# First column half of an output projection by k-pairs over four banks, with two seven-product chunks mixed into the residual

## What is computed

```python
y = jnp.concatenate([y_ret, y_mla, y_gm], axis=2)
y = rms_norm(y, mix_norm.reshape(N_MIX_HEADS, HEAD_DIM)).reshape(B, S, D_MIX)
y = jnp.concatenate([y[..., :RET_WIDTH] * jax.nn.silu(r_g), y[..., RET_WIDTH:]], axis=-1)
x = x + y @ w_out                      # 256 x 2048 @ 2048 x 2048
h = rms_norm(x, ffn_norm)
return x + (jax.nn.silu(h @ w_gate) * (h @ w_up)) @ w_down
```

## Time and profile before

| | us |
|---|---|
| median of 3 runs | 1089.78 (1089.72 to 1089.99) |
| the profiled execution | 1089.62 |
| its span | 1087.5 |
| busy in the span: PE | 1076.9 |
| busy in the span: DVE | 911.0 |
| busy in the span: ACT | 653.2 |

### The profile page before, as it was taken

The page is one execution under the profiler, slowest core; times in us unless marked ns, Lnnn a source line. Parts: engine busy times, 40 slices in busy tenths (PEclk is TensorE's granted clock), DMA queues, the critical chain, the costliest instruction groups (busy, mean ns, idle before and its releaser), DMA issues.

```text
span 1087.5 us, 12417 instructions
## 1 busy us (share of the span) xinstructions
PE 1076.9 (99%) x5094; PEld 897.1 (82%) x5094; DVE 911.0 (84%) x859; ACT 653.2 (60%) x638; POOL 55.4 (5%) x54
## 2 busy tenths in 40 slices
PE   9999999999999999999999999999999999999997
PEld 6888889987888877888888888888888888888886
DVE  6889666754576799999999999999999899989994
ACT  7666546655755566655656656566665655565653
POOL 0087000000000000000000000000000000000000
PEclk9999999999999999999999999999999999999999
DMA  8766544654355578677677677677684676655562
GB/s 327 281 212 227 192 135 133 205 161 147 117 189 167 188 271 271 198 233 243 216 232 229 209 237 222 226 232 221 229 246 155 208 257 242 202 205 202 194 198 111
DMA packets 50440, 227.50 MB, mean 209 GB/s; under 512 B 4305, under 2 KB 10193, under 8 KB 28753
## 3 DMA queue, kind: packets, MB, share of 16 engines
q1 hardware_dynamic: 48224, 214.89, 57.9%
q0 software_dynamic: 1440, 10.49, 4.7%
q10 hardware_dynamic: 720, 1.34, 0.3%
HBM read 222.51 MB, written 4.19 MB: 208 GB/s over the span
## 4 chain that ended last, share of the span: by engine, by line
PE 93%; DVE 3%; DMA 2%; ACT 1%; issue 0%; SPq 0%; DVEq 0%; ACTq 0%
PE ps L1680 72%; PE ps L1533 5%; PE ps L1535 5%; PE ps L1534 5%; PE ps L1572 2%; DMA d_raw<-in_w_gu 1%; PE ps L1620 1%; PE ps L1799 1%; PE ps L1800 1%; PE ps L1801 1%; DMA raw<-in_w_out 0%; PE ps L1619 0%; DMA raw<-in_w_i 0%; DVE ps L1375 0%; PE ps L1591 0%
## 5 line engine op out<-in xcount | busy, mean ns | idle before, releaser
L1680 PE MATMUL ps<-w_hi,xp_hi 128*128 128x512 f32 x404 | 159.6, 395 | 1.5 <-DVE ps L1375 1.0
L968 DVE TENSOR_TENSOR w_lo<-raw,w_hi 128x2048 fp32r<-128x2048 f32 (+2 forms) x42 | 87.3, 2078 | 84.1 <-ACT w_hi L493 84.1
L1680 PE MATMUL ps<-w_hi,xp_lo 128*128 128x512 f32 x404 | 157.5, 390 | 0.0
L1680 PE MATMUL ps<-w_lo,xp_hi 128*128 128x512 f32 x404 | 157.3, 389 | 0.0
L753 ACT ACTIVATE t_hi<-t_sum 128x2048 fp32r<-128x2048 f32 x44 | 84.4, 1919 | 69.9 <-DVE t_sum L1262 69.9
L836 ACT ACTIVATE w_hi<-raw 128x2048 fp32r<-128x2048 f32 (+1 forms) x44 | 79.1, 1798 | 77.6 <-DMA raw<-in_w_dn 77.6
L1680 PE MATMUL ps<-w_hi,xo_hi 128*128 128x512 f32 x292 | 113.9, 390 | 0.0
L1680 PE MATMUL ps<-w_lo,xo_hi 128*128 128x512 f32 x292 | 113.6, 389 | 0.0
L1680 PE MATMUL ps<-w_hi,xo_lo 128*128 128x512 f32 x292 | 113.6, 389 | 0.0
L1272 DVE TENSOR_TENSOR t_lo<-t_sum,t_hi 128x2048 fp32r<-128x2048 f32 x44 | 100.7, 2289 | 6.7 <-ACT t_hi L753 6.7
L493 ACT ACTIVATE w_hi<-raw 128x2048 fp32r<-128x2048 f32 (+2 forms) x42 | 73.0, 1739 | 53.0 <-DMA raw<-in_w_out 25.7
(11 more groups left out here) (294 smaller groups left out, 2446.0 us busy)
## 6 DMA issues: line engine op xcount, KB each, us to landing
raw<-in_w_gu SPq DMA_DIRECT2D x78, 1024.0 KB, 5.0
raw<-in_w_dn SPq DMA_DIRECT2D x44, 1024.0 KB, 4.8
raw<-in_w_i SPq DMA_DIRECT2D x21, 1024.0 KB, 4.8
raw<-in_w_out SPq DMA_DIRECT2D x16, 1024.0 KB, 5.1
raw<-in_w_in SPq DMA_DIRECT2D x12, 1024.0 KB, 5.1
d_raw<-in_w_gu SPq DMA_DIRECT2D x10, 1024.0 KB, 4.9
d_lo<-in_w_gu POOLq DMA_DIRECT2D x10, 1024.0 KB, 11.5
raw<-in_w_in SPq DMA_DIRECT2D x8, 576.0 KB, 3.8
```

Of the source, the lines that this page charges most:

```text
L968: nc.vector.tensor_tensor(w_lo[n % 4][:, 0:k, 0:c], raw[n % 4][:, 0:k, 0:c], w_hi[n % 4][:, 0:k, 0:c].bitcast(F32), ALU.subtract).then_inc ...
L1680: mm = nc.tensor.matmul(out, x, wt, start=start and j + m == 0, stop=stop and 3 * j + m == n - 1, skip_group_check=resumed)
```

## The change

The chunks 50 to 57, which before were the column blocks 0 and 1 in turn, are now one pair of k-tiles each, over both column blocks and both token blocks, in banks 0 to 3. The weights for them are laid out anew in memory (`w_oa`), so that a chunk's 128 rows are contiguous. Pairs 0 to 4 and 7 are plain (`out_plain`), pairs 5 and 6 (chunks 55 and 56) are seven-product chunks (`out_sums`). Their four shared products collect in banks 4 to 7. These banks are mixed in step 56 into a tile `mix_o`, and the mixture is added to `xin`, not to the banks. The chunks 58 to 65 run as before, but in banks 4 to 7. The units `xs2` and `xt2` of the feed-forward part take banks 0 to 3. In the first feed-forward chunk the order of the six early products is changed.

```diff
-OUT_ORDER = [(0, 0), (1, 0), (0, 1), (1, 1), (0, 2), (1, 2), (0, 3), (1, 3)] + [
-    (s, g) for s in (2, 3) for g in range(4)]
+O1 = O0 + FB
+OUT_SUMS = (5, 6)
+OUT_ORDER = [(s, g) for s in (2, 3) for g in range(4)]
...
-put(51, ("yt", 3), ("yt", 4), ("yt", 5))
-put(54, ("yt", 6), ("yt", 7))
+put(51, ("yt", 3), ("yt", 4), ("ys", 5))
+put(54, ("ys", 6), ("yt", 7))
...
         def unit_bank(u):
-            return bank[4 + INDEX[u] % 4]
+            return bank[INDEX[u] % 4 + (0 if u[0] in ("xt2", "xs2") else 4)]
...
+            def out_hi(n):
+                s = out_sum(n)
+                if s is None:
+                    high(n)
+                    return
+                act.wait_ge(raw_in[n % 4], 16 * (n // 4 + 1))
+                nc.scalar.activation(w_hi[n % 4][:, 1:4, :], raw[n % 4][:, 1:4, :], ACT.Copy).then_inc(hi_ready, 1)
+                act.wait_ge(in_sum_step, 3 * (in_weight_sums + s + 1))
+                nc.scalar.activation(to_hi[s][:], to_sum[s][:], ACT.Copy).then_inc(in_tops_hi, 1)
...
+            def y_sums_hi(s):
+                act.wait_ge(xi_step, 3 * (in_token_sums + s + 1))
+                nc.scalar.activation(yi_hi[s][:], yi[s][:, 4:8, :], ACT.Copy).then_inc(xi_sums_hi, 1)
+            y_sums_at = {52: 0, 55: 1}
-            x2_step = {55 + 1: 0, 57: 1, 61: 2, 65: 3}
+            x2_step = {57: 0, 58: 1, 61: 2, 65: 3}
...
+                if n in y_sums_at:
+                    y_sums_hi(y_sums_at[n])
+                if n == O0 + OUT_SUMS[-1]:
+                    act.wait_ge(in_mix_done, 5)
+                    nc.scalar.activation(mix_o[:, 0, :], bank[4], ACT.Copy).then_inc(in_mix_first, 1)
...
+            def out_lo(n):
...
+                nc.vector.tensor_tensor(to_sum[s][:, 0:2, :], raw[slot][:, 1:3, :],
+                                        b12.unsqueeze(1).to_broadcast([P, 2, COLS]), ALU.add).then_inc(in_sum_step, 1)
...
+            def y_sums(u):
...
+            def out_mix_sums():
...
+            y_sums_at = {52: 0, 55: 1}
-            out_step = {56: 0, 57: 1, 61: 2, 65: 3}
+            out_step = {61: 2, 65: 3}
             for n in range(G0, FF0):
+                if n == O1 - 1:
+                    dve.wait_ge(in_mixed, 6)
...
+                if n in y_sums_at:
+                    y_sums_lo(y_sums_at[n])
+                if n == O0 + OUT_SUMS[-1]:
+                    out_mix_sums()
...
-                    low(n + AHEAD)
+                    out_lo(n + AHEAD)
+                if n == O0 + OUT_SUMS[-1]:
+                    out_mix_x()
...
+            def out_sums(n):
...
+                shared = ((4, "a11", "b11"), (5, "n2", "t2"), (7, "s1", "t1"), (6, "s3", "t3"))
+                own = ((0, "a12", "b21"), (2, "s4", "b22"), (1, "a22", "t4"))
+                pe_.wait_ge(ys_lo, s + 1)
+                pe_.wait_ge(xi_made, in_token_sums + s + 1)
+                pe_.wait_ge(lo_ready, n + 1)
+                for out, left, right in own + shared if start else shared + own:
+                    if start and out == 4:
+                        after(unit_act, "a", ("yt", 7))
+                        after(unit_dve, "v", ("yt", 7))
...
+            for n in range(O1, FF0):
...
+                if n == O1:
+                    pe_.wait_ge(in_mix_first, 3)
+                    pe_.wait_ge(in_mix_step, 9)
...
-                for out, x, right in products[6:] if late else products[:6] if first and start else products:
-                    if first and start and out == 0:
+                if first and start:
+                    products = products[6:] if late else products[:2] + products[4:6] + products[2:4]
+                for out, x, right in products:
+                    if first and start and out in (4, 5):
+                        pe_.wait_ge(acc_free, ACC_O + out + 1)
+                    if first and start and out == 7:
                         late_units()
```

More of the change, by code:

```diff
@@ L166, in build @@
         mix_in = at("mix_in", 144 * K, [4, COLS])
+        to_sum = [at(f"to_sum{i}", 112 * K + 8 * K * i, [4, COLS]) for i in range(2)]
+        to_lo = [at(f"to_lo{i}", 112 * K + 8 * K * i, [4, COLS], F32R) for i in range(2)]
+        to_hi = [at(f"to_hi{i}", 128 * K + 8 * K * i, [4, COLS], F32R) for i in range(2)]
+        yi = [at(f"yi{i}", 64 * K + 4 * K * i, [8, P]) for i in range(2)]
+        yi_hi = [at(f"yi_hi{i}", 72 * K + 2 * K * i, [4, P], F32R) for i in range(2)]
+        yi_lo = [at(f"yi_lo{i}", 76 * K + 2 * K * i, [4, P], F32R) for i in range(2)]
+        mix_o = at("mix_o", 144 * K, [4, COLS])
         mix = at("mix", H0 + 44 * K, [4, COLS])
@@ L1284, in _ @@
                         cols = xin[:, b, s * COLS:(s + 1) * COLS]
[L1285 removed]
+                        nc.vector.tensor_tensor(cols, bank[2 * s + b][:], cols, ALU.add).then_inc(acc_free, 1)
                 if n == O0:
@@ L1817, in _, with out_plain @@
                 run_units(n)
[L1820 to L1825, removed]
+            def out_plain(n):
+                p, slot = n - O0, n % 4
+                after(unit_dve, "v", ("yt", p))
+                pe_.wait_ge(lo_ready, n + 1)
+                for side in range(4):
+                    half, b = divmod(side, 2)
+                    if p == 0 and half == 0:
+                        pe_.wait_ge(proj_free, 11 + b)
+                    elif p == 0:
+                        pe_.wait_ge(acc_free, ACC_G + 3 + b)
+                    toks, blocks = slice(b * P, (b + 1) * P), (1 - half, 3 - half)
+                    mm = group(bank[2 * half + b], [yT_hi[:, 2 * p + j, toks] for j in range(2)],
+                               [yT_lo[:, 2 * p + j, toks] for j in range(2)], [w_hi[slot][:, j, :] for j in blocks],
+                               [w_lo[slot][:, j, :] for j in blocks], p == 0, p == FB - 1)
+                    if p == FB - 1 and side < 3:
+                        mm.then_inc(in_done, 1)
+                    if side == 1 and n == MID:
+                        run_units(n)
+                mm.then_inc(chunk_used, 1)
@@ L1826, in _ @@
+            for n in range(O0, O1):
+                if out_sum(n) is None:
+                    out_plain(n)
+                else:
+                    out_sums(n)
                 if n != MID:
                     run_units(n)
+            y_made = {0: ("yt", 1), 1: ("yt", 3), 2: ("yt", 4), 3: ("yt", 7)}
+            for n in range(O1, FF0):
+                s, g = OUT_ORDER[n - O1]
+                after(unit_dve, "v", y_made[g])
+                if g >= 2:
+                    pe_.wait_ge(ys_lo, g - 1)
+                if n == O1:
+                    pe_.wait_ge(in_mix_first, 3)
+                    pe_.wait_ge(in_mix_step, 9)
+                chunk(n, yT_hi, yT_lo, range(4 * g, 4 * g + 4), 2 * s, g == 0, g == 3)
+                run_units(n)
```

118 lines of the change are left out of this document (110 added, 8 removed).

## The result

| | before | changed |
|---|---|---|
| median of the runs side by side, us | 1089.78 (1089.62 to 1090.55, 5 runs) | 1098.49 (1098.07 to 1099.61, 5 runs) |
| the profiled execution, us | 1089.62 | 1098.08 |
| its span, us | 1087.5 | 1095.6 |

The ratio is 1.0078, with a 95% interval from 1.0067 to 1.0089: the change makes the kernel 8.7 us slower. The forecast was 1097.7 in a range of 1095.1 to 1099.6.

A forecast was written before the change was run, and what follows sets the result against it. PE, busy 99% of the span, was taken as the bound. A 7.3 us wait less 1.36 saved gave +5.9, the clock +2.1: 1089.62 + 5.9 + 2.1 = 1097.6, as median 1097.7, range 1095.1 to 1099.6.

The forecast's parts named there:

- PE sets the time, and the saving is 1.36 us: Output projection: PE has no idle time; seven products instead of eight in chunks 55 and 56 save 1.36 us.
- DVE's program set out in time: DVE's instructions through steps 51 to 54, timed from rows: no pause from 311.7, reads of yt 7 done at 332.0.
- The stop: Chunk 55, after nine matmuls: PE waits before bank 4 for DVE's reads of yt 7, 7.3 us.
- The clock: Behind PE's wait in chunk 55: clock falls to its lower level, +2.1 us, between 0 and 3.
- No second stop: Chunk 56 on: mixing done by 340.7, before chunk 58; nothing more ends late, further waits taken as nothing.
- The clock holds: Rival, chunk 55: same wait but clock stays at 2.4 GHz, no slow stretch, 1095.7 us; chance 0.16.
- DVE is not late: Rival, reads of yt 7: done by 327.63 gives 1091.2 (short wait, chance 0.04), by 324.9 gives 1088.4 (covered, 0.02).
- More stops: Rival: slower preparations, or chunk 58 or units behind it wait; 1099 to 1103, chance 0.08 including a longer slow stretch.

The follow-up runs named there:

- experiment 1: Changed kernel with the new layout, banks and order but all eight pairs plain, no seven-product chunks: 1089.82 us, ratio 1.0000.
- experiment 8: Changed kernel's computation reordered: yt 7 read before the rest of chunk 56's and all of chunk 57's preparation, wait before bank 7: 1089.66 us, ratio 1.0002.
- experiment 7: The changed kernel itself, unaltered, run and profiled once more: 1099.00 us, ratio 1.0082.
- experiment 3: Changed kernel with yt 7 read ahead of pair 6's token sums, the wait before bank 4 being for both: 1096.76 us, ratio 1.0062.
- experiment 4: Changed kernel with the wait for yt 7 moved from before bank 4 to before bank 7: 1098.13 us, ratio 1.0074.
- experiment 5: Changed kernel without the two DVE instructions making the lo part of the weight sums, so its result is not the layer's: 1096.64 us, ratio 1.0061.
- experiment 2: Changed kernel with 31 extra matmuls put before the wait for yt 7 to keep PE at work: 1096.97 us, ratio 1.0064.
- experiment 6: Changed kernel with 16 or 23 extra matmuls before the wait for yt 7: 1098.46 us (ratio 1.0076) and 1098.69 us (1.0077).

## Why the prediction was right, step by step

- **PE sets the time, and the saving is 1.36 us.** Shown by experiments 1 and 8: with the layout alone nothing changes, and with the stop gone the stretch is 1.0 us shorter, the 1.36 less a wait of 0.2 and the slower matmuls behind it. What I left out is that such a saving need not last: in the medians of experiment 8, 0.6 of it is left at the end of the span and nothing in the device time.
- **DVE's program set out in time.** The prediction had `to_sum` at 312.3 and 320.5 and the reads of yt 7 done at 332.0. The trace has 312.12, 320.36 and 331.89. Every duration came from a row of the kernel before, and twenty instructions added up to an error of 0.1 us. As a time of day that is partly luck, for in experiment 7 the same program has everything 0.8 us later. Counted from the start of chunk 55 it is not: the restart was put at 9.35 us, and it came at 9.47 in both profiles. This works because DVE waits for almost nothing in these 20 us; an estimate by average load (DVE had 29 us to spare) would have said that there is no problem.
- **The stop.** 7.3 us forecast at nine matmuls into chunk 55, 7.14 measured there. DVE's lateness is 4.3 of it (its reads end at 331.89 instead of 327.63); the other 2.8 is that PE now asks earlier. Experiments 3 to 5 confirm its cause from three sides: fewer items before DVE's reads, the wait put later, less work on DVE. In each the restart moved as DVE's reads did, and stayed where only PE's order was changed.
- **The clock.** Taken at +2.1 from the start of the kernel; 2.2 measured, and 2.07 by experiment 2. The step from "PE comes from standing" to "PE has stood for 7 us" held. That the size fits so well is luck: the forecast took 4.5 us of slow matmuls from the start of the kernel, and the 4.5 behind this restart are what was left of a low stretch of 6.8 us, 2.3 of which had passed. The same program gave 1.6 in experiment 7, and the other kernels 1.6 to 2.9. The fall that the Trainium skill warns of for idle gaps in the middle of a kernel ("TensorE: Matmul & The Clock Gate", "Why this matters for your kernels") took place here, where PE stood 4.26, 5.56, 5.78, 7.14 and 7.15 us; in the profiles with 1.95 and 3.51 us it did not.
- **No second stop.** The mixing ended at 342.96 and chunk 58 came at 347.15, as predicted (347.3). The part behind it took 748.4 against 748.3 us.
- **The rivals.** "The clock holds" falls by the intervals of 0.43 us. "DVE is not late" falls by its timeline; experiment 8, where DVE reads yt 7 in time, ended at the kernel before's time and not near 1088.4, for the reasons given there. "More stops" does not show in the profile of the changed kernel, but its twin, waits in the feed-forward part that come and go, showed in experiments 5, 6 and 8.

The forecast was 0.8 us low by the median. Of this, 0.1 is the sum inside the span (+8.1 measured, +8.0 predicted). About 0.4 lies outside the span: the profiled execution is 2.5 us longer than its span, where I had carried over the 2.12 of the kernel before. In all executions with seven-product chunks in this place that part is 2.36 to 2.75 us, in all without them 2.04 to 2.16. What it consists of the profile does not show, and no run was spent on it. The remainder is that the median lies 0.4 above the profiled execution, where before it lay 0.16 above, and the clock's share and the waits in the feed-forward part, which vary as the table shows, can account for that. That they do is not shown.

## What to carry to other kernels

Before an engine with idle time on average is given more work, set its program out in time with durations from the trace and ask for the one moment at which somebody waits for it; here 29 us of spare time hid a stop of 7 us. A wait in the middle of a chunk for "all units up to the last" is as late as the latest reader, so the reader should stand before the new preparation, not behind it. Where the effect is near 1 us, compare a stretch between two marks on the bounding engine rather than the medians.

## What was not expected of the hardware

- The clock fell while PE still stood, 3.5 to 4.8 us after its last matmul in the five profiles, and was then down for 6.8 us in four of them and 3.4 in the fifth. How long PE runs at 1.2 GHz behind a stop is what is left of this at the restart: 4.5 and 3.2 us with the same program and the same stop (7.14 and 7.15 us), 5.9 and 5.8 us behind shorter stops (5.56 and 5.78 us). A shorter stop therefore bought less than its own length.
- A row of 40 slices hardly shows a fall of this size: one 8 among 9s in the changed kernel, and no mark at all in experiment 5, where the intervals at the restart are 0.43 us as well. Windows of 1 or 2 us around the stop show it, and so do the intervals between matmuls.
- A matmul that waited starts the next one later even with the clock up, 0.31 us behind it instead of 0.227 (332.48 to 332.79 in experiment 6), and 0.56 with the clock down (332.03 to 332.59). The 0.31 also stands behind the first matmul of a chunk that follows 128x128 turns without a wait (322.56 to 322.87).
